# A gated delta recurrence inside a weight-streaming decoder layer: chunk values taken as one solve of (beta v − beta k state), three steps a chunk, and the output norm in the next head's first steps

## The reference, cut to what matters

```python
k_beta = k * beta[..., None];  v_beta = v * beta[..., None]
a_mat = jnp.where(strict, jnp.einsum('bhncd,bhnsd->bhncs', k_beta, k) * decay, 0.0)
rhs = jnp.concatenate([v_beta, k_beta * jnp.exp(gc)[..., None]], axis=-1)
sol = lax.linalg.triangular_solve(a_mat + eye, rhs, left_side=True, lower=True)
u_val, w_cum = sol[..., :dv], sol[..., dv:]
def step(state, xs):                       # one chunk
    q_i, k_i, u_i, w_i, qk_i, gl_i = xs
    v_new = u_i - w_i @ state
    o_i = q_i @ state + qk_i @ v_new
    state = state * gl_i + k_i.T @ v_new
    return state, o_i
# after all chunks: o = rms_norm(o, o_norm) * silu(z)
```

## Time and profile before

| | us |
|---|---|
| median of 3 runs | 1107.88 (1107.77 to 1107.97) |
| the profiled execution, its time | 1107.9 |
| its span, first to last instruction | 1105.8 |
| TensorE busy / ScalarE / VectorE / GpSimd | 1085.3 / 469.0 / 340.6 / 553.6 |

### The profile page before, as it was taken

One profiled execution on the slowest core, in us unless ns is written; L12 is line 12 of the kernel. 1 busy time (PEld: TensorE's weight loads), 2 busy tenths in 40 slices (PEclk: granted clock), 3 DMA queues, 4 the chain that ended last, 5 costly groups with the idle time before them and its releaser, 6 DMA issues.

```text
span 1105.8 us, 20346 instructions
## 1 busy us (share of the span) xinstructions
PE 1085.3 (98%) x8312; PEld 920.4 (83%) x8312; DVE 340.6 (31%) x594; ACT 469.0 (42%) x1027; POOL 553.6 (50%) x478
## 2 busy tenths in 40 slices
PE   7999999999999999999999999999999999999996
PEld 6899999999989898978788888878888888888884
DVE  6344545455454536361100112221112121200002
ACT  5555656474656464652522323443333333322221
POOL 4353534445354536353543645655555555554551
PEclk9999999999999999999999999999999999999998
DMA  4121212221212212121432222222222322222222
GB/s 179 61 95 60 85 60 68 78 68 60 87 59 68 79 58 69 60 76 58 170 97 95 95 96 94 91 87 94 93 95 95 96 95 95 96 96 95 95 76 76
DMA packets 27788, 95.45 MB, mean 86 GB/s; under 512 B 2984, under 2 KB 3240, under 8 KB 27696
## 3 DMA queue, kind: packets, MB, share of 16 engines
q1 hardware_dynamic: 26496, 91.77, 25.4%
q10 hardware_dynamic: 1200, 2.38, 0.6%
HBM read 92.03 MB, written 2.11 MB: 85 GB/s over the span
## 4 chain that ended last, share of the span: by engine, by line
PE 91%; ACT 4%; DVE 2%; issue 1%; POOL 1%; DVEq 0%; ACTq 0%; POOLq 0%
PE bank L890 91%; DVE o_lo L679 1%; ACT w_hi L364 1%; ACT L613 1%; DVE qkv L652 0%; DVE h L885 0%; PE bank L961 0%; POOL w_lo L283 0%; ACT cbuf L364 0%; ACT nwt L496 0%; ACT am L366 0%; DVE cv L652 0%; ACT qo_hi L364 0%; DVE x_lo L656 0%; ACT sqm L367 0%
## 5 line engine op out<-in xcount | busy, mean ns | idle before, releaser
L283 POOL TENSOR_TENSOR w_lo<-w_raw,w_hi 128x512 fp32r<-128x512 f32 x324 | 428.6, 1341 | 493.5 <-ACT w_hi L364 492.7
L890 PE MATMUL bank<-x_hi,w_hi 128*128 128x264 f32 (+1 forms) x896 | 249.3, 336 | 4.4 <-DVE x_lo L656 3.7
L364 ACT ACTIVATE w_hi<-w_raw 128x512 fp32r<-128x512 f32 x324 | 190.4, 624 | 107.1 <-PE bank L890 106.7
L890 PE MATMUL bank<-x_lo,w_hi 128*128 128x264 f32 (+1 forms) x896 | 231.3, 316 | 0.0
L890 PE MATMUL bank<-x_hi,w_lo 128*128 128x264 f32 (+1 forms) x896 | 230.9, 316 | 0.0
L890 PE MATMUL bank<-og_hi,w_hi 128*128 128x512 f32 x416 | 164.7, 396 | 0.0
L890 PE MATMUL bank<-og_lo,w_hi 128*128 128x512 f32 x416 | 164.3, 395 | 0.0
L890 PE MATMUL bank<-og_hi,w_lo 128*128 128x512 f32 x416 | 164.3, 395 | 0.0
L890 PEld LDWEIGHTS bank<-x_hi,w_hi 128*128 128x128 f32 x896 | 147.4, 189 | 19.8 <-issue 3.8
L890 PEld LDWEIGHTS bank<-x_hi,w_lo 128*128 128x128 f32 x896 | 147.5, 189 | 11.3
L890 PEld LDWEIGHTS bank<-x_lo,w_hi 128*128 128x128 f32 x896 | 147.9, 189 | 8.5
(11 more groups left out here) (240 smaller groups left out, 1285.2 us busy)
## 6 DMA issues: line engine op xcount, KB each, us to landing
w_raw<-w_stream SPq DMA_DIRECT2D x162, 512.0 KB, 3.3
h_in<-h_t SPq DMA_DIRECT2D x4, 528.0 KB, 5.0
h<-h_t ACTq DMA_DIRECT2D x1, 2048.0 KB, 10.1
out<-h SPq DMA_DIRECT2D x8, 256.0 KB, 2.1
h_in<-gc_dram SPq DMA_DIRECT2D x7, 264.0 KB, 3.1
cst<-consts SPq DMA_DIRECT2D x1, 512.0 KB, 8.0
h_in<-gc_dram ACTq DMA_DIRECT2D x1, 264.0 KB, 3.0
sm<-small SPq DMA_DIRECT2D x1, 80.5 KB, 6.2
```

Of the source, the lines that this page charges most:

```text
L283: nc.gpsimd.tensor_tensor(w_lo[:, n % 2, at], w_raw[:, n % 3, at], w_hi[:, n % 2, at].bitcast(f32), ALU.subtract).then_inc(wlo_ready, 1)
L364: return nc.scalar.activation(to, x, ACT.Copy)
L890: return nc.tensor.matmul(o, w, x, start=start, stop=stop)
```

## The change

The new value of a chunk, v_new = u − w·state, is computed as one solve: r = beta·v − (beta·decay·k)·state first, then v_new = `um`·r. So:

- `kbe`, `nwt`, `w_done` and the four products of step 15 are gone, with four of the eight ScalarE copies of k and the negating copy. `be` is negated once at the start.
- The normalized k goes to a tile of its own, `kn`.
- A chunk takes three steps. Steps 14, 17, 20, 23: `kn`·`state` and `state`·`qdec`; VectorE forms r in `vb` (line 757 of the new file). Steps 15, 18, 21, 24: `um`·`vb`; ScalarE copies it into `vnew`. Steps 16, 19, 22, 25: the products with `vnew`; VectorE updates `state` at 16, 19, 22.
- The meta state product moves from step 14 to 13, the turning of k from step 0 to 7, `kdec` from 1 to 8, q·k from step 1 to 2 (and its scaling from 2 to 3), each into another bank.
- The output norm: square at 26, add at 26, round at 27, `o_lo` at 27; the sums at step 0 of the next head, behind the k·k products; the root at step 0, `xd` at 5, `og_hi` at 6, `og_lo` at 7. A ninth round of 8 steps (`TRAIL`) does this for the last head.

The diff, cut to its core (step 21's wait on `vn_ready` is not in it: the lines stay as they are):

```diff
@@ GpSimd, delta_steps
+                        if step == 7 and h >= 1:
+                            pool.wait_ge(oghi_ready, h)
+                            nc.gpsimd.tensor_tensor(og_lo[:, h - 1, :], flat(xd), og_hi[:, h - 1, :].bitcast(f32),
+                                                    ALU.subtract).then_inc(oglo_ready, 1)
@@ ScalarE, delta_steps
+                        if step == 0 and h >= 1:
+                            act.wait_ge(o_sums, h)
+                            inverse_root(flat(osq), dbank[0][:, :], 1.0, 1).then_inc(o_root, 1)
-                        if step == 1:
+                        if step == 8:
                             act.wait_ge(k_turned, h + 1)
-                            for to, factor, first in ((kbe, be, 0), (kdec, erev, 1)):
-                                for j in range(NJ):
...
-                        if step == 15:
-                            act.wait_ge(w_done, h + 1)
-                            nc.scalar.activation(flat(nwt), dbank[0][:, :], ACT.Copy, scale=-1.0).then_inc(nwt_ready, 1)
+                        if 15 <= step <= 24 and step % 3 == 0 and h >= 0:
+                            act.wait_ge(vn_done, NJ * h + (step - 15) // 3 + 1)
+                            copy(vnew[:, :], dbank[1][:, 0:128]).then_inc(vn_ready, 1)
...
-                        if 16 <= step <= 22 and step % 2 == 0 and h >= 0:
-                            act.wait_ge(vn_done, NJ * h + (step - 16) // 2 + 1)
-                            copy(vnew[:, :], dbank[1][:, 0:128]).then_inc(vn_ready, 1)
...
-                        if step == 24 and h >= 0:
+                        if step == 26 and h >= 0:
                             act.wait_ge(o_done, h + 1)
-                        if step == 25 and h >= 0:
+                        if step == 27 and h >= 0:
                             act.wait_ge(o_added, h + 1)
@@ VectorE, delta_steps
+                        if step == 5 and h >= 1:
+                            dve.wait_ge(o_root, h)
+                            link(nc.vector.scalar_tensor_tensor(flat(xd), dbank[3][:, :], on_scaled[:, 0:1], flat(osq), ALU.mult,
+                                                                ALU.mult))
+                            dve.wait_ge(zs_ready, h)
+                            mult(flat(xd), flat(xd), zs[:, (h - 1) % 2, :]).then_inc(ogf_ready, 1)
...
+                        if 14 <= step <= 23 and step % 3 == 2 and h >= 0:
+                            j = (step - 14) // 3
+                            dve.wait_ge(vb_ready, h + 1)
+                            dve.wait_ge(ks_done, NJ * h + j + 1)
+                            nc.vector.scalar_tensor_tensor(vb[:, j, :], dbank[0][:, 128 * j:128 * (j + 1)], be[:, j, h:h + 1],
+                                                           vb[:, j, :], ALU.mult, ALU.add).then_inc(r_ready, 1)
+                        if 16 <= step <= 22 and step % 3 == 1 and h >= 0:
+                            j = (step - 16) // 3
...
+                        if step == 26 and h >= 0:
+                            dve.wait_ge(o_squared, h + 1)
+                            dve.wait_ge(q_squared, h + 1)
+                            nc.vector.tensor_tensor(flat(osq), flat(osq), qsq[:, h % 2, :], ALU.add).then_inc(o_added, 1)
                         if step == 27 and h >= 0:
...
+                            dve.wait_ge(o_high, h + 1)
+                            low_part(o_lo, osq, qo_hi).then_inc(o_split, 1)
@@ TensorE, delta_steps, step 0
                             pe.wait_ge(vb_ready, h + 1)
-                            for j in range(NJ):
-                                ins = turn(dbank[0][:, c128[j]], kh[:, tok[j]], ident)
-                            ins.then_inc(k_turned, 1)
-                        if step == 1:
+                            if h:
+                                pe.wait_ge(o_split, h)
+                                spread_sums(dbank[0], flat(qo_hi), flat(o_lo)).then_inc(o_sums, 1)
+                        if step == 2:
@@ TensorE, delta_steps, the chunks
-                        if step == 15:
-                            pe.wait_ge(u_updated, len(LEVELS) * (h + 1))
-                            for j in range(NJ):
-                                ins = mm(dbank[0][:, c128[j]], kbe[:, j, :], um[:, j, :])
-                            ins.then_inc(w_done, 1)
...
+                            pe.wait_ge(state_ready, NJ * h + j + 1)
+                            mm(dbank[0][:, c128[j]], kn[:, j, :], state[:, :]).then_inc(ks_done, 1)
+                            mm(dbank[3][:, c128[j]], state[:, :], qdec[:, j, :], stop=False)
+                        if 15 <= step <= 24 and step % 3 == 0 and h >= 0:
+                            j = (step - 15) // 3
...
-                            mm(dbank[1][:, 0:128], um[:, j, :], vb[:, j, :], stop=False)
-                            mm(dbank[1][:, 0:128], nwt[:, j, :], state[:, :], start=False).then_inc(vn_done, 1)
-                            mm(dbank[3][:, c128[j]], state[:, :], qdec[:, j, :], stop=False)
-                        if 17 <= step <= 23 and step % 2 and h >= 0:
-                            j = (step - 17) // 2
+                            pe.wait_ge(r_ready, NJ * h + j + 1)
+                            mm(dbank[1][:, 0:128], um[:, j, :], vb[:, j, :]).then_inc(vn_done, 1)
+                        if 16 <= step <= 25 and step % 3 == 1 and h >= 0:
+                            j = (step - 16) // 3
                             pe.wait_ge(vn_ready, NJ * h + j + 1)
-                        if step == 26 and h >= 0:
-                            pe.wait_ge(o_split, h + 1)
-                            if nxt < HEADS:
-                                pe.wait_ge(k_root, nxt + 1)
-                            spread_sums(dbank[2], flat(qo_hi), flat(o_lo)).then_inc(o_sums, 1)
```

More of the change, by code:

```diff
@@ L106, in hybrid_block_kernel @@
         qdec = sb("qdec", tile4, f32, mix_mem)
-        nwt = sb("nwt", tile4, f32, mix_mem)
-        osq = nwt
-        pbx = nwt
+        osq = sb("osq", tile4, f32, mix_mem)
+        pbx = osq
         sqm = sb("sqm", [128, META], f32, mix_mem)
@@ L442, in delta_steps @@
             def delta_steps():
-                for h in range(-1, HEADS):
+                for h in range(-1, HEADS + 1):
                     nxt = h + 1
-                    for step in range(0 if h >= 0 else PRE, STEPS):
+                    for step in range(0 if h >= 0 else PRE, STEPS if h < HEADS else TRAIL):
+                        if step == 0 and h >= 1:
+                            act.wait_ge(o_sums, h)
+                            inverse_root(flat(osq), dbank[0][:, :], 1.0, 1).then_inc(o_root, 1)
+                        if step == 6 and h >= 1:
+                            act.wait_ge(ogf_ready, h)
+                            copy(og_hi[:, h - 1, :], flat(xd)).then_inc(oghi_ready, 1)
+                        if h == HEADS:
+                            yield
+                            continue
                         if h < 0 and step == 22:
@@ L745, in delta_steps @@
                                                            ALU.mult, ALU.add).then_inc(state_ready, 1)
-                        if step == 24 and h >= 0:
-                            dve.wait_ge(o_squared, h + 1)
-                            dve.wait_ge(q_squared, h + 1)
-                            nc.vector.tensor_tensor(flat(osq), flat(osq), qsq[:, h % 2, :], ALU.add).then_inc(o_added, 1)
-                        if step == 25 and h >= 0 and nxt == HEADS:
-                            dve.wait_ge(o_high, h + 1)
-                            low_part(o_lo, osq, qo_hi).then_inc(o_split, 1)
                         if nxt < HEADS:
@@ L944, in delta_steps @@
                 qh, kh, vh = qkv[:, 0, :], qkv[:, 1, :], qkv[:, 2, :]
-                for h in range(-1, HEADS):
+                for h in range(-1, HEADS + 1):
                     nxt = h + 1
-                    for step in range(0 if h >= 0 else PRE, STEPS):
+                    for step in range(0 if h >= 0 else PRE, STEPS if h < HEADS else TRAIL):
+                        if h == HEADS:
+                            if step == 0:
+                                pe.wait_ge(o_split, h)
+                                spread_sums(dbank[0], flat(qo_hi), flat(o_lo)).then_inc(o_sums, 1)
+                            yield
+                            continue
                         if step == 0:
@@ L959, in delta_steps @@
                             pe.wait_ge(vb_ready, h + 1)
-                            for j in range(NJ):
-                                ins = turn(dbank[0][:, c128[j]], kh[:, tok[j]], ident)
-                            ins.then_inc(k_turned, 1)
-                        if step == 1:
+                            if h:
+                                pe.wait_ge(o_split, h)
+                                spread_sums(dbank[0], flat(qo_hi), flat(o_lo)).then_inc(o_sums, 1)
+                        if step == 2:
```

(9 more changed lines are left out.)

83 lines of the change are left out of this document (35 added, 48 removed).

## The result

The changed kernel takes 1112.11 us (1112.01 to 1112.19, 5 runs) against 1107.88 (1107.77 to 1108.27, 5 runs) before: 1.0037 times as long, 95% interval 1.0026 to 1.0049, or 4.2 us slower. The forecast was 1112.1. The span grew from 1105.8 to 1110.1 us.

A forecast was written before the change was run, and what follows sets the result against it. The prediction took TensorE, busy 98% of the span, as the bound. Its terms, −7.1 − 4.0 + 4.4 + 2.3 + 8.6 = +4.2 us on 1107.9, gave 1112.1 us; own range 1110.2 to 1115.0, 8-in-10 range 1105.0 to 1116.0.

The forecast's parts named there:

- Part 1: Step 15: the four products of w go, freeing 0.89 us of TensorE's stream in each of 8 heads, −7.1 us.
- Part 2: TensorE's old wait for `o_lo` at the output-norm sums goes, 0.57 us in each of 7 heads, −4.0 us.
- Part 3: Step 21: the `sqm` product newly waits for the third `vnew`, 0.63 us in each of seven heads, +4.4 us.
- Part 4: Step 22: `k_lo` loses its turn to GpSimd's `w_lo`, k sums wait 0.32 us in seven heads, +2.3 us.
- Part 5: Step 0: sums wait for `o_lo`, 1.23 us a head with the add held (0.73 without), seven times, +8.6 us.
- A: Rival, no change: VectorE ahead of GpSimd at step 22 and the add not held, 1106.3 us; chance 0.24.
- B: Rival, faster: step 21's wait stays, step 0's sums and `k_lo` wholly hidden, 1101.2 us; chance 0.16 together with D.
- D: Rival: old wait left, nothing added, only the removed w products count, 1100.8 us; chance 0.16 together with B.
- C: Rival, much slower: both halves of `w_lo` pass ahead of `k_lo` at step 22, 1121.1 us; chance 0.08.

The follow-up runs named there:

- experiment 7: The kernel before with only one of the four w products of step 15 (output not the reference's): 1102.41 us.
- experiment 8: The kernel before with its output-norm sums at step 27 instead of 26: 1106.33 us.
- Experiment 1: The changed kernel with the `sqm` product and its copy moved from step 21 to step 22: 1105.76 us.
- experiment 3: The changed kernel with ScalarE's k root of step 24 taken ahead of the fourth `vnew` copy: 1104.17 us.
- Experiment 2: The changed kernel with VectorE's `k_lo` taken at step 21 instead of 22: 1110.44 us.
- experiment 4: The changed kernel with ScalarE's second half of the weights in block u made at quarter 3 instead of 2: 1111.12 us.
- experiment 6: The changed kernel with the output-norm sums and ScalarE's root moved from step 0 to step 1 of the next head: 1116.19 us.

## Why the prediction was right, term by term

- **Part 1** (−7.1): experiment 7 gives 0.22 us a product, so 7.1.
- **Part 2** (−4.0): in experiment 8 the old wait is worth 0.59 us in head 0, and 0.49 in the others beside a new wait for `um` of about 0.1. The 0.57 of the forecast stands.
- **Part 3** (+4.4): the `sqm` product came 0.75 behind its forerunner and the stream 0.24 behind that, where 0.22 and 0.15 were the undisturbed distances: 0.62 a head, 4.3. Experiment 1 removes it (with part 4's term), experiment 3 leaves it in place.
- **Part 4** (+2.3): `k_lo` 1.71 us, the k sums late by 0.28, 2.0. Experiment 2 gives back 1.7 in the time and 1.95 in the trace. (The forecast's 7 × 0.32 is 2.2, not 2.3; nothing hangs on it.)
- **Part 5** (+8.6): 1.17 a head, 8.2; experiment 3 gives back 7.9. That the add is held was the choice on which 3.5 us hung. It took 1.17 us beside a `w_lo` and 0.67 without, in experiment 4, and the cost a head changed by 0.5, as the two values 1.23 and 0.73 said. The Trainium skill (SBUF — State Buffer, "Who interferes with whom") has this as a rule for a VectorE instruction with two SBUF inputs beside a GpSimd one that reads SBUF; the trace agrees for the add, `k_lo` (1.71 us against 0.69), `tm` (0.80 against 0.43) and the tap (1.81).

With part 2 at its 4.0, the terms as measured sum to +3.4 us, and the span grew by 4.3. Of the 0.9 left, 0.35 is one wait at step 4 of head 0, the `xt` line of the waits (between the stream products behind step 3 and those behind step 4 lie 2.40 us, 2.05 before): this head has no sums at step 0 that would hold TensorE back. It is the wait that experiments 4 and 6 brought to six and eight heads, and the forecast did not have it. Another 0.34 lies behind the recurrence, between the wait for `w_lo` after the last head and 735.5 us of the span (193.73 us against 193.38 before). There each stretch of 24 products with `x_hi` and `x_lo` takes 5.60 us instead of 5.57 to 5.58, while those with other operands take 5.60 in both kernels. The rest comes in pieces of under 0.05 a head. For the last two I cannot name the cause.

So every mechanism of the forecast was there, and each term was within 0.4 us of its size. That the forecast of 1112.1 met 1112.11 is luck in the last microsecond: the three costs were put 0.8 too high together (15.3 against 14.5), and 0.9 that the forecast did not have made up for it.

What the forecast took each for by itself and was in truth coupled: what stands at step 21, and who gets the turn at step 22. The sum was right, since the wait, the product and the hold were all there. It would have been wrong for a version with the first of them cured, as the expectation for experiment 1 was. The rivals: A would have needed `k_lo` to win its turn and the add to slip in, and both were held; B and D would have needed the boundary to be covered, and it was 1.17 us a head short; C did not come, since GpSimd's second half waited for `k_lo` (the two halves took 2.99 us together).

## What to carry to other kernels

Work saved on the engine that bounds the kernel (7.1 us here) is kept only where everything behind its new, shorter schedule is in time. So walk each chain that starts at a moved instruction through every engine to the one that waits, and look at what stands in front of the chain's first link: three small moves here (a root ahead of a copy, a product one step later, `k_lo` one step earlier) made 1112.1 into 1097.3 us. Moving the product that waits by a step pays only where what stands behind it has room. It did for `sqm` (experiment 1), and in the recurrence for the old output sums (3.55 of 4.0 us in experiment 8), but not for the new ones (0.4 of about 8 in experiment 6). It can cost in the one place, start or end, where the pattern is different, as it did in both 6 and 8.

## What was not expected of the hardware

- Which of VectorE and GpSimd gets its turn is decided by very little: where `k_lo` starts 0.05 us ahead it takes 0.68 us, and 0.13 behind, 1.71. When it wins, `w_lo` pays (1.77 us instead of 1.29), and nobody waits for that.
- The VectorE instruction that was held gets the next turn: `k_lo` got in between two `w_lo` whose inputs were both ready, in all seven heads.
- The last head is not like the others: two function table loads of 1.28 us lie around its root, ahead of weight halves. One step more for its sums cost 1.3 us more of waiting in experiment 8 and 2.7 in experiment 6 (3.2 against 0.5), which no row of heads 0 to 6 foretells.
- A single long wait can cost more than its length. After 3.6 us without a product in experiment 6 the granted clock was 0.50 for some 3.3 us, and the products took 1.5 us more. After 0.9 us (changed kernel) and 2.3 us (experiment 8, 533.31 to 535.66) at the same place the granted clock stayed at 1.00.
